# Moving the softmax normalisation of a windowed attention branch into the merge stage, with the denominators kept in DRAM

## The reference

```
logits = q . k * hd**-0.5 - slope * |i - j|      for |i - j| <= 128
p      = exp(logits - m)
denom  = sum(p) + exp(sink - m)
out_A  = (p @ v) / denom
```

```
z = sum_b sigmoid(gate_b) * (out_b @ w_branch_b)
x = x + z @ w_out
x = x + relu(RMSNorm(x) @ w_up)**2 @ w_down
```

## Time and profile before

| what | value |
|---|---|
| median of the runs shown | 3394.64 us (2 runs, 3393.75 to 3395.54) |
| profiled execution, its own time | 3398.46 us |
| span of its slowest core (core 7) | 3396.9 us |
| spans of the eight cores | 3363.4 to 3396.9 us |
| TensorE busy in the span | 2719.8 us (80%) |
| VectorE busy | 1460.0 us (43%) |
| ACT busy | 1204.2 us (35%) |
| branch A, first score matmul to last product | 1385 to 1609 us of the span |
| merge, first load to last store | 2044 to 2430 us of the span |

### The profile page before, as it was taken

The page is one execution under the profiler, slowest core; times in us unless marked ns, Lnnn a source line. Parts: engine busy times, 40 slices in busy tenths (PEclk is TensorE's granted clock), DMA queues, the critical chain, the costliest instruction groups (busy, mean ns, idle before and its releaser), DMA issues.

```text
span 3396.9 us, 46062 instructions; the slowest of 8 cores (3363.4 to 3396.9 us)
## 1 busy us (share of the span) xinstructions
PE 2719.8 (80%) x14116; PEld 1291.9 (38%) x14116; DVE 1460.0 (43%) x2393; ACT 1204.2 (35%) x2158; POOL 292.8 (9%) x277
## 2 busy tenths in 40 slices
PE   3498889998889997465553646999469999999998
PEld 2253334433334443232253533444234444444443
DVE  5367885378860000355255564555221122212221
ACT  6235551045453332587763640222121122112210
POOL 0100000000000000000023234444200000000000
PEclk9999999999999998799986867988789999999999
DMA  7522223322223413511394847665591011101110
GB/s 223 62 75 75 63 63 96 96 69 63 74 76 95 104 75 105 123 40 37 116 255 131 252 131 223 235 236 180 154 168 62 5 58 63 62 17 46 63 50 25
DMA packets 262523, 352.21 MB, mean 104 GB/s; under 512 B 32400, under 2 KB 220560, under 8 KB 254352
## 3 DMA queue, kind: packets, MB, share of 16 engines
q1 hardware_dynamic: 224288, 306.27, 27.3%
q0 software_dynamic: 38000, 42.99, 8.9%
HBM read 262.21 MB, written 130.02 MB: 115 GB/s over the span
## 4 chain that ended last, share of the span: by engine, by line
PE 64%; ACT 13%; DVE 7%; DMA 6%; issue 6%; POOL 2%; another core or an unknown queue 1%; SPq 1%; ACTq 1%; DVEq 0%; POOLq 0%
PE p_acc L410 17%; PE p_acc L1085 13%; PE p_upp L1072 13%; PE p_acc L421 6%; PE p_ybr L935 5%; DVE t_stg L481 4%; PE p_acc L957 4%; ACT t_lnb L464 3%; ACT t_lnb L462 2%; ACT t_E L556 2%; PE p_N L577 2%; DMA t_ksl<-sKB 2%; DMA t_wt<-w_in 1%; PE p_Dn L577 1%; ACT t_rD L645 1%
## 5 line engine op out<-in xcount | busy, mean ns | idle before, releaser
L410 PE MATMUL p_acc<-t_hT,t_wt 128*128 128x512 bf16 x3712 | 847.9, 380 | 98.5 <-DVE t_stg L481 81.4
L410 PEld LDWEIGHTS p_acc<-t_hT,t_wt 128*128 128x128 bf16 x3712 | 345.3, 97 | 592.2 <-issue 218.1
L1072 PE MATMUL p_upp<-t_h2Tt,t_wup 128*128 128x512 bf16 x2048 | 445.7, 380 | 38.1 <-DMA t_wup<-w_up 38.1
L1085 PE MATMUL p_acc<-t_wdn,t_upT 128*128 128x512 bf16 x2048 | 445.6, 380 | 38.0 <-DMA t_wdn<-w_down 25.8
L1076 ACT ACTIVATE t_rl<-p_upp 128x512 f32<-128x512 f32 x256 | 153.1, 598 | 758.1 <-PE p_upp L1072 751.3
L462 ACT ACTIVATE t_lnb<-p_ssp 128x512 f32<-128x512 f32 x276 | 165.0, 598 | 541.0 <-PE p_ssp L460 526.7
L1077 DVE TENSOR_TENSOR t_upT<-t_rl 128x512 bf16<-128x512 f32 x256 | 177.4, 693 | 310.6 <-ACT t_rl L1076 310.6
L1085 PEld LDWEIGHTS p_acc<-t_wdn,t_upT 128*128 128x128 bf16 x2048 | 200.4, 98 | 283.2 <-issue 44.7
L1072 PEld LDWEIGHTS p_upp<-t_h2Tt,t_wup 128*128 128x128 bf16 x2048 | 200.9, 98 | 281.6 <-issue 43.2
L481 DVE SCALAR_TENSOR_TENSOR t_stg<-p_acc,t_par,t_lnb 128x512 bf16<-128x512 f32 x272 | 248.3, 913 | 82.5 <-ACT t_lnb L464 79.3
L556 ACT ACTIVATE t_E<-p_S 128x512 bf16<-128x512 f32 (+3 forms) x548 | 217.2, 453 | 149.9 <-PE p_S L542 136.9
(11 more groups left out here) (87 smaller groups left out, 2456.9 us busy)
## 6 DMA issues: line engine op xcount, KB each, us to landing
t_xt<-x SPq DMA_DIRECT2D x16, 2048.0 KB, 10.5
sGT<-t_stg SPq DMA_DIRECT2D x24, 1024.0 KB, 3.9
t_gTt<-sGT SPq DMA_DIRECT2D x8, 3072.0 KB, 21.5
t_wt<-w_in POOLq DMA_DIRECT2D x17, 1024.0 KB, 13.9
y<-t_xt SPq DMA_DIRECT2D x8, 2048.0 KB, 6.8
t_x<-y SPq DMA_DIRECT2D x8, 2048.0 KB, 7.8
y<-t_x SPq DMA_DIRECT2D x8, 2048.0 KB, 6.6
sKB<-t_stg SPq DMA_DIRECT2D x12, 1024.0 KB, 4.0
```

Source lines behind the costliest of these rows:

```text
L410: i = h.matmul(a[:, :], lhsT=w[:, kc, u["wcol"]:u["wcol"] + 128], rhs=rhs[:, kc, t * TT:(t + 1) * TT], start=(kc == 0), stop=(kc == 7))
L1072: ins = h.matmul(U[:, :], lhsT=wup[:, kc, c * 128:(c + 1) * 128], rhs=hT_[:, kc, :], start=(kc == 0), stop=(kc == 7))
L1085: ins = h.matmul(A[:, :], lhsT=upT[:, c, s * 128:(s + 1) * 128], rhs=wdn[:, c, half * 512:(half + 1) * 512], start=(c == 0), stop=(c == 31))
```

## The change

`a_post` no longer normalises. It copies the raw numerators from p_N to t_ost with two copies on VectorE, copies the raw denominators from p_Dn to t_rD (on ACT in even groups, on VectorE in odd ones), and stores the two valid quarters of t_rD to a new DRAM tensor sDA of 32-bit numbers. The sink, the logarithm, the exponential and the product move to the merge stage, into a new function `p3_norm_a(t)`, which loads 1 MB of denominators for a tile into the single buffer DAt, takes four logarithms of 512 columns and one exponential of 2048 columns on ACT in place, and multiplies the first four blocks of t_oTt by the result on VectorE in place. It stands after the loads of tile 0 and of tile 1, ahead of the first merge step, and for tile t+2 after the merge steps of step 2 of tile t.

```diff
@@ DRAM tensors @@
+    DA = dt_s("sDA", [4, 128, NT], F32)
@@ a_post @@
-                cx.op(act, lambda h: h.activation(out=r_[:], in_=dbk[:, :], func=AF.Ln,
-                                                  bias=par[:, P_SINKE + c:P_SINKE + c + 1]),
-                      reads=[b_dbank[gi % 2], b_par], writes=[br])
-                cx.op(act, lambda h: h.activation(out=r_[:], in_=r_[:], func=AF.Exp, scale=-1.0), reads=[br], writes=[br])
-                cx.op(dve, lambda h: h.tensor_tensor(out=o_[0:64, c, 0:QTA], in0=nb[0:64, 0:QTA], in1=r_[0:64, 0:QTA],
-                                                     op=ALU.mult),
-                      reads=[b_nbank[gi % 2], br], writes=[bo])
-                cx.op(dve, lambda h: h.tensor_tensor(out=o_[64:128, c, 0:QTA], in0=nb[64:128, QTA:2 * QTA],
-                                                     in1=r_[64:128, QTA:2 * QTA], op=ALU.mult),
-                      reads=[b_nbank[gi % 2], br], writes=[bo])
+                q0 = qt * QTA
+                cx.op(dve, lambda h: h.tensor_copy(out=o_[0:64, c, 0:QTA], in_=nb[0:64, 0:QTA]),
+                      reads=[b_nbank[gi % 2]], writes=[bo])
+                cx.op(dve, lambda h: h.tensor_copy(out=o_[64:128, c, 0:QTA], in_=nb[64:128, QTA:2 * QTA]),
+                      reads=[b_nbank[gi % 2]], writes=[bo])
+                if gi % 2 == 0:
+                    cx.op(act, lambda h: h.activation(out=r_[:], in_=dbk[:, :], func=AF.Copy),
+                          reads=[b_dbank[gi % 2]], writes=[br])
+                else:
+                    cx.op(dve, lambda h: h.tensor_copy(out=r_[:], in_=dbk[:, :]), reads=[b_dbank[gi % 2]], writes=[br])
+                cx.dma(sp, None, DA[c, 0:64, q0:q0 + QTA], r_[0:64, 0:QTA], reads=[br])
+                cx.dma(sp, None, DA[c, 64:128, q0:q0 + QTA], r_[64:128, QTA:2 * QTA], reads=[br])
@@ merge stage @@
+        DAt = sb(p3, "DAt", [128, 4, TT], F32)
+        b_DAt = Buf("DAt")
...
+        def p3_norm_a(t):
+            i = t % 2
+            cx.dma(sp, None, DAt[:], DA[:, :, t * TT:(t + 1) * TT].rearrange("c p t -> p c t"), writes=[b_DAt])
+            for c in range(4):
+                cx.op(act, lambda h: h.activation(out=DAt[:, c, :], in_=DAt[:, c, :], func=AF.Ln,
+                                                  bias=par[:, P_SINKE + c:P_SINKE + c + 1]),
+                      reads=[b_DAt, b_par], writes=[b_DAt])
+            cx.op(act, lambda h: h.activation(out=DAt[:], in_=DAt[:], func=AF.Exp, scale=-1.0),
+                  reads=[b_DAt], writes=[b_DAt])
+            cx.op(dve, lambda h: h.tensor_tensor(out=oTt[i][:, 0:4, :], in0=oTt[i][:, 0:4, :], in1=DAt[:], op=ALU.mult),
+                  reads=[b_oTt[i], b_DAt], writes=[b_oTt[i]])
...
         p3_og_loads(0)
         p3_x_loads(0)
+        p3_norm_a(0)
         p3_og_loads(1)
+        p3_norm_a(1)
         for dc in range(8):
             merge_step(0, dc)
...
                 if nxt:
                     for dc in msched[s_]:
                         merge_step(t + 1, dc)
+                if s_ == 2 and t + 2 < NTT:
+                    p3_norm_a(t + 2)
```

## The result

The changed kernel is slower: the ratio of its time to that of the kernel before is 1.007, with a 95% interval of 1.0056 to 1.0084 (medians 3423.26 and 3395.59 us over all runs). That is about 24 us more, where 8 less were forecast. The profiled execution took 3419.55 us: outside the forecast's own range (3368 to 3406), inside the wider one (3353 to 3424). Run once more beside its variants it gave 1.0081 (1.0059 to 1.0104).

What follows compares the result with a forecast made beforehand. Branch A was taken as bound by a closed circle of waits, the merge by TensorE. Terms -59 (branch A), +37 (merge start) and +14 (tiles) gave -8 us: 3390.5 us profiled, own range 3368 to 3406, 8-in-10 range 3353 to 3424.

Steps and rivals of the forecast that it cites:

- the circle of Ln, Exp, product, mask and p_Dn: Branch A: a closed chain of waits, not a full engine, sets the group period of 3.47 us.
- the 3416 and 3417 us of two rivals: Branch A: odd copies cost fully, period 3.0, 3416 us (13%); merge tiles: denominators land late, 3417 us (10%).
- Gain: 64 x (3.475 - 2.55) = 59 us.: Branch A: the group period falls from 3.475 to 2.55 us over 64 groups, 59 us faster.
- The stretch with the odd copy: Branch A: odd groups take 2.75 us, with the denominators' copy on VectorE; even groups take 2.3 us.
- I cost the stores at nothing; the cover is 1.4 us thick.: Branch A: t_rD is free 3.1 us after the copy and wanted after 4.5, so the denominators' stores cost nothing.
- about 8 us of SP: Branch A: eight store issues, the t_qtz load pair and t_ost's store occupy SP about 8 of 10.2 us per four groups.
- The rival with stores that land one after the other: Branch A: each group's two stores serialise, 4.6 us becomes the period, +72 us there, 3518 us in all (3%).
- The first gate product starts 37 us late.: Merge start: two normalisations, the second awaiting its load into the single DAt, precede the first gate product: 37 us.
- what is left, 2.3 us, goes straight into the exposed wait: Merge tiles: the normalisation delays step 3's additions, so the last transposes wait 2.3 us longer; six times, 14 us.
- late-denominators rival: Merge tiles: denominators land 7.2 us later, ACT waits 5.0 us, 7.3 us a tile, 44 in all, 3417 us (10%).
- one of the signs that I had named for being wrong: Merge tiles: the prediction is wrong if ACT waits for DAt there.
- DA lands 2.2 + 8/6 = 3.5 us later than I say: Merge tiles: the denominators' load landing 3.5 us later than forecast would turn the forecast gain of 8 us into a loss.

Runs made afterwards that it cites:

- e6: Kernel before the change, with branch A's whole normalisation issued one item later and nothing moved to the merge: ratio 0.9918.
- e3: Changed kernel without the merge-stage normalisation, with all denominators copied on ACT instead of every other group's: ratio 0.9889, branch A 193.5 us.
- e1: Changed kernel with only branch A's part, the normalisation calls in the merge stage taken out: ratio 0.9906, branch A 197.2 us.
- e2: Changed kernel without the merge-stage normalisation and without the stores of the denominators: branch A 188.2 us, no ratio.
- m3: Changed kernel with tile 1's normalisation behind the merge steps of tile 0 instead of ahead of them: ratio 1.0002.
- m2: Changed kernel with the denominators of tile t+2 loaded ahead of its outputs and gates: ratio 1.0036, seven tiles 290.2 us.
- m4: Changed kernel with denominators loaded early, tile 1's normalisation behind tile 0's merge steps and the product at the tile's end: ratio 0.995.

## Why the prediction was wrong

The bound was read rightly: the circle of Ln, Exp, product, mask and p_Dn set branch A's pace. e6 opens it by order alone and has 30 of the 33 us that the change has there. The structure of the sum (a gain in branch A, a price at the start and one in each tile) held too. The sign was missed because terms were mis-sized: the gain in branch A above all, the stores, which were put at nothing, and the price of a tile. The time is near the 3416 and 3417 us of two rivals, but that is chance, since neither came about as described: the period was 2.78 us and not 3.0, and in the tiles ACT waited for denominators 7.6 us in all at most (core 5 of the repeat) and not 5.0 in each.

- **"Gain: 64 x (3.475 - 2.55) = 59 us."** It was 33. The period is 2.78 us, 44 us of gain in the steady state (0.695 x 64); the stores of the next point take most of the rest. The stretch with the odd copy took 2.66 us where I had 2.75, the one without took 2.90 where I had 2.3, so the longer stretch is not the odd one, as I had said, but the other. I worked out each stretch for itself and left TensorE's work over a whole pair out, since it was busy only 136 of 224 us. But it stops 1.09 us for the odd copy, then has the work of two groups to catch up with, and VectorE waits for it in the other stretch: TensorE's 4.3 us of work and its stop make 5.4 of the pair's 5.56 us. e3 shows that 0.6 of it hangs on the odd copy; the rest of this account is read from the trace, and no run tests it alone.
- **"I cost the stores at nothing; the cover is 1.4 us thick."** They cost 9 us (e1 against e2). I worked out the cover for the steady state, where it holds; what I left out are the two ends. In the first groups the stores that ACT waits for take 3 to 8 us to land where I had 2.3, and SP waits for slow t_qtz loads; at the end the barrier waits for the last store. (The "about 8 us of SP" are 6.5 by the figures beside them; measured issues of 0.45 and 0.60 us for the two stores of a group make them 8.) The rival with stores that land one after the other did not come about: the steady pair of groups is the same with and without them, and each lands 2.1 us after its issue. The Trainium skill, "DMA: Bandwidth & Descriptors", section "Rules for kernel authors", advises against two transfers to disjoint partition halves because they serialise. The trace does not show that here: the two halves are issued 0.5 us apart and land 0.6 us apart. Whether one store of 128 partitions would be cheaper no run shows.
- **"The first gate product starts 37 us late."** 37.1 by the medians of the cores (34.5 on core 0 against core 7 of before). m3 shows 16.5 of them to be the second normalisation. This step was right.
- **"what is left, 2.3 us, goes straight into the exposed wait"** The mechanism is right and the size was 2.9 us, as m2 has it in each of its tiles: 17 us instead of 14. m4 moves the product and gets it all back. The row that I read is of core 7, where the w_out products of step 3 took 4.36 us at a granted clock of 0.81; on core 1 of m2 they take 3.62 us, so the additions are due 0.7 us earlier, and 2.3 becomes 3.0.
- **The rest of the tiles.** In the result's trace the seven tiles took 303.4 us, 13 more than with the product's place alone (m2). Part is the late-denominators rival in a small form: ACT waited 5.9 us for them on core 0, and 7.6 on core 5 of the repeat. So one of the signs that I had named for being wrong, ACT waiting for DAt in the tiles, did appear. m2 removes it. The other part is TensorE's clock, which the sum held constant. Windows over four tiles (span, busy us of each engine, granted clock, DMA share, GB/s): core 0 before, core 7 before, core 1 of m2, core 0 of the changed kernel:

```profile
2137.00:2304.00 167.00, 152.23 (x767) 72.22 (x765) 104.54 (x144) 43.27 (x80) 80.32 (x64) 0.95 0.72 238
```

```profile
2136.40:2311.10 174.70, 160.22 (x767) 74.11 (x766) 104.92 (x144) 43.37 (x80) 80.33 (x64) 0.90 0.67 228
```

```profile
2144.00:2322.00 178.00, 151.53 (x766) 72.29 (x765) 112.39 (x147) 62.06 (x100) 80.37 (x64) 0.92 0.74 245
```

```profile
2131.00:2325.00 194.00, 161.48 (x764) 74.50 (x763) 113.88 (x148) 62.35 (x100) 80.79 (x64) 0.87 0.74 225
```

The two effects come apart. TensorE's idle time, 14.8 and 14.5 us before, is 26.5 in m2 with its stops of 6.6 us and 32.5 in the changed kernel, where stops reach 10 us: that is the change's. Its busy time for the same matmuls is 152 us in the first and third window and 160 to 161 in the other two, and one of these is the kernel before, with stops of 3.6 us. In these two the granted clock falls to 0.81 in stretches of 5 to 15 us between the stops; in the other two it does not. So the 9 us of longer work on core 0 need no longer stop and are not shown to be the change's. After the longer stop the same matmuls take no longer (151.5 us in m2), though the stretch at half clock (1.2 GHz) around it grows from 3.4 us (core 0 before) to 6.8 (core 2 of the repeat). Why all cores of the result's trace and two of the kernel before's were granted less is open.

The point that I gave for a change of sign ("DA lands 2.2 + 8/6 = 3.5 us later than I say") assumed the other terms to hold. With 26 us less in branch A the sign turned without it.

## What to carry to other kernels

When an engine that is not full seems to bound a stage, look for the closed circle of waits, and first try to open it by order: one item's delay of the normalisation (e6, 28 us) was worth more than moving the work to another stage, even in the best order tried there (m4, 17 us). Work that is moved must be placed in each in-order queue: the same product cost 2.9 us a tile ahead of the additions that TensorE waits for, and nothing behind them. And when a forecast is a difference of two terms of 50 us, their errors decide its sign.

## What the hardware showed that I had not expected

- The same store of 256 KB (t_ost to sOT) held SP's queue 0.36 us in the kernel before and in e2, and 0.58 us in the median (core 0) in the changed kernel, where the stores of the denominators stand around it; of those, 64 KB each, the first of a group took 0.45 us to issue and the second 0.60. So the size does not set it. What does, no run shows.
- Transfers of one queue do not always land in the order of issue: on core 0 of the changed kernel the load of t_qtz issued at 1389.86 us landed at 1396.10, the store issued at 1390.53 landed at 1395.43. At the start of the merge they did land in order, as the prediction took it.
- A Ln of 64x256 took 0.47 us and the next one, independent of it, started 0.49 us after it, while one of 128x512 takes 0.69: half the columns on half the partitions, two thirds of the time.
- The clock granted to TensorE over the seven tiles lay between 0.88 and 0.92 in the changed kernel, its repeat, m2 and m3, and between 0.89 and 0.95 in the kernel before; the seven tiles took 289 to 308 us in the former and 277 to 289 in the latter.
